# Two-block transformer layer pair in fp32r parts: the key projection of the second self-attention in 512-column matmuls

## What is computed

```python
h = rms_norm(x, pre_mix_g[l])
z = h @ w_in[l]
za, zb, zc = z[..., :split_a], z[..., split_a:split_b], z[..., split_b:]
q, k, v = jnp.split(zb, 3, axis=-1)
q, k, v = (a.reshape(Bn, S, B_HEADS, HEAD_DIM).transpose(0, 2, 1, 3) for a in (q, k, v))
yb = moba_attention(q, k, v)
yc = conformer_conv(zc, w_dw[l], b_dw[l], conv_gn_g[l], conv_gn_b[l])
```

## Time and profile before

| | us |
|---|---|
| median of three runs | 773.35 |
| the profiled execution | 773.14 |
| its span, first to last instruction | 771.9 |
| TensorE busy | 760.2 (98%) |
| VectorE busy | 582.1 (75%) |
| ScalarE busy | 443.5 (57%) |
| GpSimd busy | 76.4 (10%) |

### The profile page before, as it was taken

The page is one execution under the profiler, slowest core; times in us unless marked ns, Lnnn a source line. Parts: engine busy times, 40 slices in busy tenths (PEclk is TensorE's granted clock), DMA queues, the critical chain, the costliest instruction groups (busy, mean ns, idle before and its releaser), DMA issues.

```text
span 771.9 us, 11259 instructions
## 1 busy us (share of the span) xinstructions
PE 760.2 (98%) x4342; PEld 656.4 (85%) x4342; DVE 582.1 (75%) x804; ACT 443.5 (57%) x666; POOL 76.4 (10%) x134
## 2 busy tenths in 40 slices
PE   6999999999999999999999999999999999999997
PEld 5998777888898888888899997789988888888885
DVE  5889999889896676686677998667757756665664
ACT  6567687865665444444474487567646644444452
POOL 5033930000200000000020001110001100000001
PEclk9999999999999999999999999999999999999999
DMA  9999988765466676856557554446434655666651
GB/s 323 367 284 327 363 306 310 255 196 167 134 204 227 213 260 204 299 186 203 181 154 238 160 173 137 138 163 219 137 110 136 216 191 193 190 194 190 190 165 55
DMA packets 84132, 161.29 MB, mean 209 GB/s; under 512 B 5408, under 2 KB 15968, under 8 KB 84080
## 3 DMA queue, kind: packets, MB, share of 16 engines
q1 hardware_dynamic: 82656, 157.31, 62.1%
q10 hardware_dynamic: 992, 2.78, 1.1%
q0 software_dynamic: 432, 0.49, 0.3%
HBM read 159.51 MB, written 1.05 MB: 208 GB/s over the span
## 4 chain that ended last, share of the span: by engine, by line
PE 95%; DVE 2%; DMA 1%; issue 1%; SPq 0%; POOL 0%; ACT 0%; DVEq 0%; POOLq 0%; ACTq 0%
PE bank L2050 18%; PE bank L2051 18%; PE bank L2052 18%; PE bank L2140 15%; PE bank L2143 8%; PE bank L2112 5%; PE bank L2063 2%; PE bank L2070 1%; PE bank L2065 1%; PE bank L2523 1%; PE bank L2193 1%; PE bank L2338 1%; DMA ada_ring<-in_w_ada 1%; PE bank L2361 1%; DVE ada_acc L1136 1%
## 5 line engine op out<-in xcount | busy, mean ns | idle before, releaser
L1104 DVE TENSOR_TENSOR lo_ring<-raw_ring,hi_ring 128x1024 fp32r<-128x1024 f32 x247 | 302.3, 1229 | 133.5 <-ACT hi_ring L568 132.8
L568 ACT CAST hi_ring<-raw_ring 128x1024 fp32r<-128x1024 f32 x248 | 259.8, 1052 | 241.8 <-PE bank L2052 127.1
L2050 PE MATMUL bank<-hi_ring,branch_hi 128*128 128x512 f32 x352 | 138.4, 393 | 0.0
L2051 PE MATMUL bank<-lo_ring,branch_hi 128*128 128x512 f32 x352 | 137.2, 390 | 0.0
L2052 PE MATMUL bank<-hi_ring,branch_lo 128*128 128x512 f32 x352 | 137.0, 389 | 0.0
L2140 PE MATMUL bank<-h_hi_lo,hi_ring 128*128 128x512 f32 x512 | 128.1, 392 | 0.0
L2140 PEld LDWEIGHTS bank<-h_hi_lo,hi_ring 128*128 128x128 f32 x512 | 92.9, 189 | 17.2
L2052 PEld LDWEIGHTS bank<-hi_ring,branch_lo 128*128 128x128 f32 x352 | 66.1, 188 | 14.0
L2050 PEld LDWEIGHTS bank<-hi_ring,branch_hi 128*128 128x128 f32 x352 | 66.2, 188 | 13.6 <-issue 0.6
L2051 PEld LDWEIGHTS bank<-lo_ring,branch_hi 128*128 128x128 f32 x352 | 66.2, 188 | 13.1 <-issue 0.2
L2143 PEld LDWEIGHTS bank<-h_hi_lo,lo_ring 128*128 128x128 f32 x512 | 69.8, 190 | 5.0
(11 more groups left out here) (332 smaller groups left out, 1179.1 us busy)
## 6 DMA issues: line engine op xcount, KB each, us to landing
raw_ring<-in_w_ff SPq DMA_DIRECT2D x128, 512.0 KB, 3.6
raw_ring<-in_w_in SPq DMA_DIRECT2D x64, 512.0 KB, 4.9
raw_ring<-in_w_out SPq DMA_DIRECT2D x16, 512.0 KB, 3.4
raw_ring<-in_w_xkv SPq DMA_DIRECT2D x16, 512.0 KB, 3.5
mem_v<-in_w_ada SPq DMA_DIRECT2D x13, 512.0 KB, 5.6
mem_k<-in_w_ada SPq DMA_DIRECT2D x11, 512.0 KB, 5.7
ada_ring<-in_w_ada SPq DMA_DIRECT2D x8, 512.0 KB, 7.2
raw_ring<-in_w_branch SPq DMA_DIRECT2D x8, 512.0 KB, 3.3
```

The lines of the kernel that those rows point to most:

```text
L568: act.copy(m.hi[:, m.slot(u)], m.raw[:, m.slot(u)]).then_inc(s.hi_done, 1)
L1104: dve.tensor_tensor(m.lo[:, m.slot(u)], m.raw[:, m.slot(u)], as_f32(m.hi[:, m.slot(u)]), ALU.subtract).then_inc(s.lo_done, 1)
L2050: pe.matmul(out, a_hi, b_hi, start=start, stop=False, skip_group_check=True)
L2051: pe.matmul(out, a_hi, b_lo, start=False, stop=False, skip_group_check=True)
```

## The change

The keys are made as the queries are, by `unit_both`, in banks 0, 1, 6 and 7. ScalarE copies the upper halves (`take_parts`, twice 512 elements, two banks at a time) in place of the whole banks, and VectorE adds the lower halves (`add_parts`, two instructions) and signals `k2_out`. On VectorE the adds stand ahead of lo of unit 145, behind the taps of the third K2 unit; the taps beside the fourth K2 unit fall from four to two, and those beside the first two units of `MEM_V0` rise from four and three to five and four.

```diff
-MIX_B_BANKS, Q2_BANKS = (0, 2), (2, 4)
+MIX_B_BANKS, Q2_BANKS, K2_BANKS = (0, 2), (2, 4), (0, 6)
...
     for j in range(RING):
         if j == RING - 1:
-            take_half(K2 + RING, 0, pair(m.kT, 0), s.k2_out)
-            take_half(K2 + RING, 1, pair(m.kT, 2), s.k2_out)
+            take_parts(K2 + RING, K2_BANKS, m.kT, s.k2_part)
         after(K2 + j)
...
     for j in range(2 * RING):
         if j == RING:
             add_parts(s.q2_part, Q2_BANKS, m.qT, s.q2_out)
+        if j == 2 * RING - 1:
+            add_parts(s.k2_part, K2_BANKS, m.kT, s.k2_out)
         after(Q2 + j)
-        conv_taps(5 if j < RING else 4)
+        conv_taps(5 if j < RING else 4 if j < 2 * RING - 1 else 2)
...
     for j in range(RING):
         follow(10 + j)
         after(MEM_V0 + j)
-        conv_taps((4, 3, 0, 0)[j])
+        conv_taps((5, 4, 0, 0)[j])
...
-    claim(0, 1)
+    claim(0, 1, 6, 7)
     for j in range(RING):
-        features(K2 + j, j, m.h_hi, m.h_lo, 0)
-    free[0] = free[1] = s.k2_out, 2
+        unit_both(K2 + j, UK * j, m.h_both, K2_BANKS, j == 0, j == RING - 1).then_inc(s.used, 1)
+    for i, b in enumerate(K2_BANKS):
+        free[b] = free[b + 1] = s.k2_out, i + 1
```

More of the change, by code:

```diff
@@ L320, in __init__ @@
         self.glu, self.glu_sig = new("glu"), new("glu_sig")
-        self.q2_part, self.q2_out, self.k2_out, self.v2_out = new("q2_part"), new("q2_out"), new("k2_out"), new("v2_out")
+        self.q2_part, self.q2_out, self.v2_out = new("q2_part"), new("q2_out"), new("v2_out")
+        self.k2_part, self.k2_out = new("k2_part"), new("k2_out")
         self.gelu_u, self.gelu_v, self.u_ok = new("gelu_u_in"), new("gelu_v"), new("gelu_u")
```

## The result

The changed kernel takes 776.81 us (median of five executions: 775.19, 776.35, 776.81, 776.93, 776.94), the kernel before 773.11 us in the same comparison. The ratio is 1.0041, with a 95% interval from 1.0029 to 1.0052: slower by 0.4%, clear of the 0.2% that the prediction took as the limit. The time lies above the range that was given (774.4 to 776.1 us).

The account below looks back on a forecast made before the run. TensorE, busy for 98% of the span, was taken to bound the kernel. 1.57 + 0.40 = +1.97 us on 773.14 us gave 775.11 us, 775.3 us on the median; forecast 775.2 us, range 774.4 to 776.1 us.

Parts of the forecast that it names:

- Part 1: Four units of keys on TensorE: fewer, wider matmuls make them 0.35 us shorter together, which only lengthens the later pause.
- Part 2: First scores: TensorE waits 1.92 us for VectorE's late adds of the keys, so the scores come 1.57 us later.
- Part 3: Two moved taps in MEM_V0: the first costs nothing, the second delays TensorE's turn2(3) by 0.40 us.
- The sum: Whole kernel: 1.57 + 0.40 = +1.97 us, giving 775.11 us on the profile's own time; chance 0.62.
- rival 3: After the pause at the scores TensorE's clock falls, matmuls take twice their pitch, 2 us lost: 777 us; chance 0.04.
- Rival 1: Only the pause at the scores is paid, the second moved tap is covered: 774.7 or 774.9 us; chance 0.16.
- Rival 4: At the convolution's normalisation a later hand-over also breaks, by some 0.4 to 0.6 us: 775.7 us; chance 0.10.
- Rival 2: VectorE's adds end by 442.0 us, TensorE does not stop at the scores: 772.8 to 773.2 us; chance 0.08.

Follow-up runs that it names:

- the second trace: Trace of a 776.6 us execution from running the changed kernel again with no edit; that set's median was 776.67 us, ratio 1.0043.
- the run with the old keys: Kernel before, with its three-pass keys; only the copies of their two banks moved from ScalarE to VectorE, where the change has its adds: 774.76 us, ratio 1.0026.
- the trace with the pause of 3.1 us: Changed kernel with the keys' adds moved behind lo of unit 145 in VectorE's queue: median 777.93 us over four executions.

## Why the prediction was wrong

**Part 1 held.** The four units of keys take 439.08 - 427.91 = 11.17 us, as foretold. The 0.08 us that was set beside the 0.35 us was no fair rival: the Trainium skill, page "TensorE: Matmul & The Clock Gate", section "Back-to-back issue gap", gives that gap for a single matmul by itself and says that in a stream of weight loads and matmuls, as here, both set the pace.

**Part 2 held.** The adds start at 442.64 us and the scores at 444.07 us (444.00 us in the second trace); foretold were 442.64 and 443.97 us. The wait is 1.94 us, foretold 1.92 us. That the saving of part 1 would vanish in the wait is shown by the run with the old keys: with a wait shorter by 0.35 us it costs 774.76 - 773.02 = 1.7 us, about what the change's own pause costs in its executions with the full clock (775.2 us less 773.1 us and less the 0.4 us of part 3).

**Part 3 held.** turn2(3) starts at 489.82 us, foretold 489.7 us, and the taps alone cost 0.40 us in their trace.

**The sum held for two executions of ten,** 775.19 and 775.29 us beside 775.11 us.

**What failed is the dismissal of rival 3.** It was given 0.04 and left out of the range; it is what eight of ten executions do. The prediction argued that "a pause of 1.9 us is shorter than" the time for which the clock stayed full at the end of the kernel. Those rows tell when the clock fell after TensorE's last work in one execution. They don't tell that a shorter pause is safe, and the second trace shows the clock falling after a pause of 1.95 us, some 1.7 us after TensorE had gone back to work. The price was about right: some 4 us at the lower clock and 2 us lost, 777 us, were worked out; the trace has some 3.4 us there and 1.5 us lost, in the rows from 445 to 450 us, and 776.8 us was measured. With the rival as the likeliest case the forecast would have been right. The Trainium skill, page "TensorE: Matmul & The Clock Gate", section "Why this matters for your kernels", warns only of longer gaps in the matmuls than this one; here the measurement decides, with the long time in eight of ten executions after a pause of 1.9 us.

**Rival 1** fell: the second tap is paid. **Rival 4** did not show in the change, yet in four of the five experiments with early adds a later hand-over, at the reciprocals or at the convolution, did turn. **Rival 2** seems to have been priced too low: in the run nearest to it, the adds one unit earlier with the change's taps, TensorE did not stop at the scores and the time was 773.9 us, not 772.8 to 773.2 us. VectorE's 0.4 us of added load had been left out.

## What to carry to other kernels

Where the bounding engine has no waits, the work that is taken off it must be set against the load that is put on the engines beside it: 0.35 us less on TensorE cost 1.19 us on VectorE, which was just as full in this stretch, and a gain showed in a trace only when four taps, 1.58 us of VectorE's work, were moved into gaps ahead of a wait, not behind one. A pause put into a dense stream of matmuls can have a second price besides its length, the lower clock after it: here that came with a pause of 1.9 us in eight of ten executions, and with one of 1.5 us in none of eleven. Matmuls that nobody reads, put into the pause, took that price away here at no cost in time (775.03 us, beside 775.2 us in the change's executions with the full clock).

## What was not expected of the hardware

The clock fell late: it was full through the pause of 1.9 us and fell when TensorE had been at work again for some 1.7 us; in the trace with the pause of 3.1 us it fell some 0.8 us after the pause. By the times, a wait of 1.5 us brought it down in none of 11 executions, one of 1.9 us in 8 of 10. At the lower clock a 256-column matmul with its weight load takes 0.21 us in place of 0.12 us, a factor of 1.8 and not 2, so the stretch of some 3.4 us at half clock cost 1.5 us.
